# Output weights split during the last attention pair, in the room of the normed input, and the first token tile of the output projection multiplied there

## The reference

```python
# x: 1024 tokens x 1024, 16 learned meta tokens in front; everything in float32
z = rmsnorm(h, attn_norm)
q, k, v, f_logit, xc, b_gate, c_gate = split(z @ w_in)
attn = forgetting_attention(q, k, v, f_logit)          # 8 heads of 64
conv = b_gate * conv3(c_gate * xc)                      # short gated convolution, 512 wide
mixed = rmsnorm(concat(attn, conv) by groups of 64)     # 1024 wide
h = h + mixed @ w_out                                   # output projection
z = rmsnorm(h, ffn_norm)
h = h + hierarchical_moe(z)                             # 32 experts, 2 for each token
out = rmsnorm(h, final_norm)[16:]
```

## Time and profile before

| what | value |
|---|---|
| median of 3 runs | 1298.27 us (1297.89 to 1299.26) |
| the profiled execution | 1299.05 us, of which the span of the trace is 1297.1 us |
| PE, DVE, ACT busy | 1160.9, 888.4 and 738.7 us |
| block `output_projection` | 526.1 us to about 660 us of the span |
| expert block | from 660 us |

### The profile page before, as it was taken

The page is one execution under the profiler, slowest core; times in us unless marked ns, Lnnn a source line. Parts: engine busy times, 40 slices in busy tenths (PEclk is TensorE's granted clock), DMA queues, the critical chain, the costliest instruction groups (busy, mean ns, idle before and its releaser), DMA issues. The chain is left out here.

```text
span 1297.1 us, 17769 instructions
## 1 busy us (share of the span) xinstructions
PE 1160.9 (89%) x6109; PEld 907.2 (70%) x6109; DVE 888.4 (68%) x1117; ACT 738.7 (57%) x882; POOL 80.3 (6%) x135
## 2 busy tenths in 40 slices
PE   5999999999999997699949999999999999999950
PEld 3888788779878885588736667666667666676630
DVE  7445635553563454666659898888988889888838
ACT  7344444443444434522247777777777777777724
POOL 0011011011010000001200000000000000000013
PEclk8999999999999998899969999999999999999975
DMA  6145353345331000574369999999999999999928
GB/s 182 51 114 122 83 129 81 89 118 125 89 90 48 17 18 1 200 308 162 142 219 351 382 389 402 397 391 389 392 399 401 388 390 392 398 402 390 385 85 332
DMA packets 86214, 306.28 MB, mean 236 GB/s; under 512 B 14665, under 2 KB 39241, under 8 KB 61601
## 3 DMA queue, kind: packets, MB, share of 16 engines
q1 hardware_dynamic: 67680, 241.83, 49.4%
q0 software_dynamic: 11328, 38.80, 11.0%
q10 hardware_dynamic: 7168, 25.17, 5.8%
HBM read 254.36 MB, written 51.41 MB: 236 GB/s over the span
## 5 line engine op out<-in xcount | busy, mean ns | idle before, releaser
L1483 DVE TENSOR_TENSOR m_wl<-raw,m_wh 128x2048 fp32r<-128x2048 f32 x192 | 437.2, 2289 | 75.4 <-ACT m_wh L1356 73.1
L1356 ACT ACTIVATE m_wh<-raw 128x2048 fp32r<-128x2048 f32 x192 | 367.8, 1918 | 130.0 <-PE m_py L131 50.7
L129 PE MATMUL m_pg<-m_wh,m_xh 128*96 128x512 f32 x256 | 104.3, 407 | 6.2 <-DVE m_xl L1487 4.9
L143 PE MATMUL a_pj<-zh,a_wh 128*128 128x348 f32 (+1 forms) x416 | 107.6, 355 | 0.0
L143 PE MATMUL a_pj<-zl,a_wh 128*128 128x348 f32 (+1 forms) x416 | 107.5, 355 | 0.0
L143 PE MATMUL a_pj<-zh,a_wl 128*128 128x348 f32 (+1 forms) x416 | 106.4, 352 | 0.0
L129 PE MATMUL m_py<-m_wh,m_hh 128*96 128x512 f32 x256 | 103.2, 403 | 2.3 <-DVE m_hl L1512 2.3
L129 PE MATMUL m_pu<-m_wh,m_xh 128*96 128x512 f32 x256 | 102.7, 401 | 0.0
L131 PE MATMUL m_pg<-m_wh,m_xl 128*96 128x512 f32 x256 | 101.9, 398 | 0.0
L130 PE MATMUL m_pg<-m_wl,m_xh 128*96 128x512 f32 x256 | 101.6, 397 | 0.0
L130 PE MATMUL m_py<-m_wl,m_hh 128*96 128x512 f32 x256 | 101.4, 396 | 0.0
(11 more groups left out here) (241 smaller groups left out, 2107.0 us busy)
## 6 DMA issues: line engine op xcount, KB each, us to landing
raw<-in_w_gate_dram SPq DMA_DIRECT2D x64, 1024.0 KB, 10.1
raw<-in_w_up_dram SPq DMA_DIRECT2D x64, 1024.0 KB, 9.3
raw<-in_w_down_dram SPq DMA_DIRECT2D x64, 1024.0 KB, 8.7
xrows<-a_kl POOLq DMA_DIRECT2D x51, 256.0 KB, 4.9
a_raw<-in_w_in_dram SPq DMA_DIRECT2D x24, 512.0 KB, 4.1
m_xg<-xrows ACTq DMA_DIRECT2D x32, 384.0 KB, 8.2
yrows<-m_ys ACTq DMA_DIRECT2D x32, 384.0 KB, 7.0
yrows<-a_kl POOLq DMA_DIRECT2D x33, 256.0 KB, 4.9
```

Source lines behind the costliest of these rows:

```text
L129: nc.tensor.matmul(out, xh, wh, start=first, stop=False)
L143: mm = nc.tensor.matmul(out, w[:, k, 0:m], z[:, k, at:at + n], start=n_pass == 0, stop=n_pass == PASSES - 1)
L1356: nc.scalar.activation(wh[s][:], raw[j][:], ACT.Copy).then_inc(S["w_hi"], 1)
L1483: nc.vector.tensor_tensor(wl[s][:], raw[j][:], wh[s][:].bitcast(F32), ALU.subtract).then_inc(S["w_lo"], 1)
```

## The change

The split of `w_out` moves from the output block into the last pair of `mixers`, and so does the product of token tile 0. Its parts:

- The two slots `a_raw` of the mixers, free after the last projection weights are split, take the eight pieces of `w_out` one after the other (SP, issued by a wait for the slot's `out_lo`). `out_high(n)` on ACT writes piece `OUT[n]` into `zh`, `out_low(n)` on DVE the remainder into `zl`. They stand behind the split of each probability group in steps 15 and 16 (pieces 0 to 4) and behind step 16 (5, 6, 7).
- The token tile 0 of `mx` is split into `wh[0]` and `wl[0]`: the six old blocks in steps 15 and 16, the two own blocks at the end of the pair.
- `out_product(n)` on PE multiplies tile 0 by piece `OUT[n]` in six matmuls into the bank pair `pj`: 0 and 1 between the turned groups of step 16, 2 behind the spread in step 17, 3 to 7 at the end.
- `output_projection` takes `zh`, `zl`, `wh`, `wl` and `pj` over, and loads no `w_out`. Its PE begins with tile 1. Its SP now issues the six expert loads directly behind the small ones, ahead of the third tile of `o_x`; their buffers have new places.

```diff
 # mixers, SP, end of the last pair
+                    if final:
+                        for n, k in enumerate(OUT):
+                            if n < 2:
+                                sp.wait_ge(S["split_lo"], i * WT + (n + 7))
+                            else:
+                                sp.wait_ge(S["out_lo"], n - 1)
+                            sp.dma_start(out_raw(n), w_out[0, k * P:(k + 1) * P, :]).then_inc(out_in[n % 2], 16)
 # mixers, ACT
+                    def out_high(n):
+                        if final:
+                            act.wait_ge(S["projected"], i * WT + 8)
+                            act.wait_ge(out_in[n % 2], 16 * (n // 2 + 1))
+                            nc.scalar.activation(c.zh[:, OUT[n], 0:D], out_raw(n), ACT.Copy).then_inc(S["out_hi"], 1)
...
+                                if s >= STEPS - 1:
+                                    out_high(2 * (s - STEPS + 1) + a)
...
                         if s == STEPS:
+                            out_high(5)
...
+                            out_high(6)
+                            out_high(7)
...
+                    if final:
+                        act.wait_ge(S["conv_mixed"], 1)
+                        act.wait_ge(S["mixed"], i + 2)
+                        nc.scalar.activation(own_blocks(wh[0]), own_blocks(c.mx), ACT.Copy).then_inc(S["tile_hi"], 1)
 # mixers, DVE
+                    def out_low(n):
+                        if final:
+                            dve.wait_ge(S["out_hi"], n + 1)
+                            nc.vector.tensor_tensor(c.zl[:, OUT[n], 0:D], out_raw(n), c.zh[:, OUT[n], 0:D].bitcast(F32),
+                                                    ALU.subtract).then_inc(S["out_lo"], 1)
 # mixers, PE
+                    def out_product(n):
+
+                        if final:
+                            k = OUT[n]
+                            if n == 0:
+                                pe.wait_ge(S["gated"], i + 1)
+                            pe.wait_ge(S["tile_lo"], 1 if n < 6 else 2)
+                            pe.wait_ge(S["out_lo"], n + 1)
+                            for b in range(2):
+                                cols = slice(b * BANK, (b + 1) * BANK)
+                                three_passes(nc, pj[:, cols], wh[0][:, k, :], wl[0][:, k, :], c.zh[:, k, cols], c.zl[:, k, cols],
+                                             n == 0, n == KD - 1)
...
+                                if s == STEPS and a >= 1:
+                                    out_product(a - 1)
...
+                            out_product(2)
...
+                    for n in range(3, KD):
+                        out_product(n)
 # output_projection, SP
-                for k in range(SLOTS):
-                    weights(k)
                 for t in range(2):
                     sp.dma_start(xt[t][:], x[0, t * P:(t + 1) * P, :]).then_inc(x_in[t], 16)
-                for k in range(SLOTS, KD):
-                    weights(k)
...
+                for e, kind, j in [(0, 0, 2), (0, 1, 3), (0, 2, 4), (0, 3, 5), (1, 0, 0), (1, 1, 1)]:
+                    to, src = unit(c.raw[j], kind, e, w_gate, w_up, w_down)
+                    sp.dma_start(to, src).then_inc(c.raw_in[j], 16)
 # output_projection, PE
-                pe.wait_ge(S["m_lo"], 1)
-                for k in range(KD):
-                    pe.wait_ge(S["w_lo"], k + 1)
-                    for b in range(2):
-                        products(0, b, [k])
+                pe.sem_inc(S["multiplied"], 2)
```

More of the change, by code:

```diff
@@ L183, in mixers @@
         raw = [c.sb(ctx, f"a_raw{s}", [P, KD, P], F32) for s in range(2)]
-        wh = [c.sb(ctx, f"a_wh{t}", [P, KD, P], F32R) for t in range(2)]
-        wl = [c.sb(ctx, f"a_wl{t}", [P, KD, P], F32R) for t in range(2)]
+        wh, wl = c.wh, c.wl
         qs = c.sb(ctx, "a_qs", [P, 2, SEQ], F32R)
@@ L213, in mixers @@
         s3 = c.ps(ctx, "a_s3", [P, 3 * BANK])
-        pj = c.ps(ctx, "a_pj", [P, 3 * BANK])
+        pj = c.pj
         pt = c.ps(ctx, "a_pt", [P, BANK])
@@ L219, in mixers @@
                  "rden_done", "spread", "meta_kept", "o_scaled", "squared", "averaged", "rooted", "mixed", "cb_in", "taps_in",
-                 "x_copied", "u_done", "gated", "c_squared", "c_averaged", "c_rooted", "c_ln", "o_ln", "masks_made", "blanks_made", "own", "passed")
+                 "x_copied", "u_done", "gated", "c_squared", "c_averaged", "c_rooted", "c_ln", "o_ln", "masks_made", "blanks_made", "out_hi", "out_lo", "tile_hi", "tile_lo", "conv_mixed", "own", "passed")
         S = {n: c.sem("a_" + n) for n in names}
         raw_in = [c.sem(f"a_raw_in{s}") for s in range(2)]
+        out_in = [c.sem(f"a_out_in{s}") for s in range(2)]
         PIECES = 1 + NT
@@ L648, in pair @@
                                                       [P, NT, 2, HD])).then_inc(S["rden_done"], 1)
+                            for n in (5, 6, 7):
+                                out_low(n)
                             if not final:
@@ L663, in pair @@
                     dve.wait_ge(S["c_rooted"], i + 1)
-                    link(mix(cv, u, PAIRS))
+                    if final:
+                        mix(cv, u, PAIRS).then_inc(S["conv_mixed"], 1)
+                        dve.wait_ge(S["conv_mixed"], 1)
+                    else:
+                        link(mix(cv, u, PAIRS))
                     for n, (a, b) in sides(final):
@@ L1058, in place @@
                                     ALU.min).then_inc(S["placed"], 1)
[L1059 to L1064 removed]
+                dve.sem_inc(S["m_lo"], 1)
+                mix_low(1)
                 dve.wait_ge(S["made"], 1)
@@ L1180, in experts @@
         wl = [c.sb(ctx, f"{tag}_wl{s}", [P, UNIT], F32R) for s in range(RING)]
-        xg = [c.sb(ctx, f"{tag}_xg{s}", [BLK, D], F32) for s in range(2)]
         xh = [c.sb(ctx, f"{tag}_xh{s}", [P, KD * BLK], F32R) for s in range(2)]
         xl = [c.sb(ctx, f"{tag}_xl{s}", [P, KD * BLK], F32R) for s in range(2)]
+        over = c.sb(ctx, tag + "_over", [P, NE, NB_LESS], F32)
+        for j in range(UNITS):
+            c.sb(ctx, f"room_of_raw{j}", [P, UNIT], F32)
+        xg = [c.sb(ctx, f"{tag}_xg{s}", [BLK, D], F32) for s in range(2)]
         ids = [c.sb(ctx, f"{tag}_ids{s}", [BLK, 1], I32) for s in range(2)]
```

84 lines of the change are left out of this document (42 added, 42 removed).

## The result

The changed kernel takes 1305.35 us (median of 6 runs, 1304.29 to 1310.88), the kernel before 1298.04 (6 runs beside it, 1296.57 to 1299.26). The ratio is 1.0059, 95% interval 1.0044 to 1.0073: it is 0.59% slower, some 7.7 us by the ratio and 7.3 by the medians. I had forecast 1298.8 with a range up to 1302.5. The profiled execution took 1310.88, the longest of the six, and the one of the kernel before 1299.05: these two are 11.8 us apart, over 4 us more than the medians.

What follows compares the result with a forecast made beforehand. PE, busy 89% of the span, was taken as the bound, so its waits count. 15.5 us added in the last pair less 15.0 saved in the output block gave +0.5: 1298.8 us on the median, range 1293.5 to 1302.5.

Steps and rivals of the forecast that it cites:

- The tail: End of the last pair: `a_o` starts 8.8 us late, at 528.1, and the block change comes at 541.6.
- The 15.5 us added: Delay of the block change, from 526.1 to 541.6, by the added work, with five microseconds at half clock.
- the ring: Steps 15 and 16, where each turned group goes PE, ACT, DVE, PE; work put between the links delays it.
- the 3.3 us of a load: Last pair: time taken for one 512 KB load of a `w_out` piece on a quiet queue.
- What goes: Block change to tile 0's router logits (the mark): 27.57 us shrink to 12.6, so 15.0 us saved.
- second condition: Ahead of the mark, `o_wrg` waits for thirteen small loads, expected 11.5 to 12.5 us behind the block change.
- fall together: At the mark, PE's own work and the small loads are ready at about one time; 12.6 us taken.
- PE filled from there: Sign: from tile 0's logits on, PE has work without holes.
- The new buffers' places cost nothing: Output block: the moved buffers add no time.
- if PE stands for the small loads for over 2 us: Sign of being wrong, ahead of tile 0's logits: PE waits over 2 us for the thirteen small loads.
- The rival for slower: Two-slot ring: slower loads, some 2.4 us per microsecond, small loads 2 more; 1301 to 1304; chance 0.25.
- The rule that I set beside the ring: Two-slot loads: some 2.0 us fixed plus bytes, hidden only if issued early; chain 0.3 us shorter by it.

Runs made afterwards that it cites:

- e2: Changed kernel with the pieces of `w_out` landing in four places instead of two; 1304.12 us, ratio 1.0036 to the kernel before.
- e12: Changed kernel with five landing places and the splits of pieces 5 to 7 moved out of steps 15 and 16; 1299.50 us, ratio 1.0010.
- e3: Changed kernel with the six expert loads issued behind the first store of `o_z` again, as in the kernel before; 1304.29 us, ratio 1.0046.
- e8: Changed kernel with twelve small loads early, five landing places, late splits of pieces 5 to 7 and weight rows of 1024 columns; 1294.83 us, ratio 0.9962.
- e9: e8 with the high halves of the output weights starting 640 bytes further, at their old distance from the low halves; 1293.77 us, ratio 0.9966.
- e1: Changed kernel with twelve of the thirteen small loads issued in the last pair, into idle tiles; 1300.61 us, ratio 1.0008.
- e4: Changed kernel with tile 0's split and product moved back into the output block, weights still split in the last pair; 1307.59 us, ratio 1.0059.
- e11: Changed kernel with the eight loads of `o_gr` made one DMA; 1302.38 us, ratio 1.0028.
- e10: Changed kernel with the eight `o_gr` and two `o_br` loads issued ahead of the gain and the two `o_wr`; 1301.47 us, ratio 1.0020.
- e6: Changed kernel with the split weights in rows of 1024 columns instead of 1044; 1307.39 us, ratio 1.0069.
- e7: Changed kernel with twelve small loads early, four landing places and weight rows of 1024 columns; 1298.14 us, ratio 0.9990.
- e5: Kernel before with the output weights' halves in rows of 1044 columns instead of 1024; 1300.6 us, ratio 1.0011.

## Why the prediction was wrong

**The tail was right, to about 1 us.** Forecast: `a_o` near 528, block change 541.6, ACT's waits at pieces 2, 5 and 7, and a low clock behind the hole ahead of the averages. Measured: 527.86, 542.03, these waits and one more at piece 3 (0.77), the averages at 0.50 in 3.75 us. The 15.5 us added were 15.9. Counted from the previous addition of `a_o` (503.15, and 503.91 before) they were 16.7, and `a_o` was 9.3 us late where I had 8.8: the changed kernel's execution entered step 15 0.8 us early, which hides a part. Which part of the ring weighs most I had not said; e2 and e12 show it is the splits inside it more than their loads. The figures that I set beside the 3.3 us of a load, from the Trainium skill, DMA: Bandwidth & Descriptors, section Anatomy of one DMA, are there those of loads issued from GpSimd; these are issued on SP, and no term of the sum rested on them.

**The step that failed is "What goes", at its second condition:** "I expect 11.5 to 12.5, bounds 10.5 and 14.5" for the small loads, on the reasoning that eight pieces of `w_out` in front had stretched their issues. The pieces were not the cause, or not the main one. Without them the first `o_gr` is blocked for 3.79 us, and in the kernel before it was blocked nearly as long, 3.32, with the other seven at 0.43 each:

```profile
539.51 3.32 SPq L933 DMA_DIRECT2D o_gr<-in_ffn_norm_dram  x1
```

The last load lands 15.6 us behind the block change (11.3 until its issue and 4.3 to land, where the sum for "as long as before" had 10.9 and 3.6), beyond my bound, and the mark comes at 16.27 instead of 12.6: 3.7 us. PE itself was ready 10.5 us behind the block change (its last product starts at 552.16 and takes 0.39), since the clock stayed high there (1.00), so the two conditions that I let "fall together" were 5.75 us apart.

**A cost that had no term** followed from it. The stall lowered the clock to 0.50 for more than 8 us: 3.9 us more (17.84 against 13.92). I had the low level behind the block change, where it didn't come, and none behind the mark. "PE filled from there" held, at half speed.

**A cost put at nothing:** "The new buffers' places cost nothing" was wrong by some 0.2 us a tile, 1.1 us in all.

In the trace these make 15.9 - 27.57 + 16.27 = 4.6 at the mark, 3.9 and 0.2 for the clock and the first step, 1.0 until tile 7: 9.7. The medians are closer than these two executions, and what the others lost at each place no trace shows; e3, whose order of PE is the same, had a step of 16.79 and ended at 1303. The expert block is left out of this: between the last logits and the end the changed kernel's execution took 2.3 us longer than before, but with the same instructions there e8 took 2.6 us longer, e9 1.5 and e3 3.2 us less, so it varies with no visible link to the change.

My sign of being wrong, "if PE stands for the small loads for over 2 us", named the place. The rival for slower put 2 us there and most of its weight on the ring's loads; both its place and its price were off. The rule that I set beside the ring, from the Trainium skill, DMA: Bandwidth & Descriptors, section Rules for kernel authors (a load's fixed part is hidden where it is issued early and waited for late), bore more on the thirteen small loads. e1, which does that to twelve of them, agrees with 6.6 us, though most of what it takes out of the way is the time of the blocked issues (11.3 of the 15.6 us until the last one landed), which is not the fixed part.

## What to carry to other kernels

When work is taken out of a stage, list what that work covered. Thirteen small loads (0.5 to 512 KB) were free under 10.9 us of product and cost 5.75 us, and the clock behind them, when it was gone; issued some 110 us ahead of the block change, into tiles that are idle then, twelve of them are free again (e1). Splits that fill "idle" time belong behind the ring whose links wait for each other, not between them: the same three splits a few rows later were worth 0.26 to 0.28%, and places for their loads to land another 0.23%. And when an issue is seen to take eight times its usual length, find what blocks it before assuming that a change removes it.

## What the runs showed of the hardware that was not expected

- An issue on SP takes 0.43 us, but the first one behind the gain (512 KB) and the two `o_wr` (128 and 16 KB, in 1024 rows each) took 3.3 to 3.9 us in the kernel before, the changed one, e2, e3, e4, e11 and e12, whether or not `w_out` was in the queue. With the ten smallest ahead, none of the thirteen was over 1.5 us, and the load behind them took 2.28 (e10). Behind the two `o_wr` without the gain the longest took 1.60 (e1).
- A short stall was followed by a lower clock, also where PE had been full shortly before (5.00 of 5 us from 545 to 550 in e11): 1.25 us of idleness at the mark came with 1.6 us lost up to tile 1 (e11), 2.22 with 1.6 (e10), 2.89 with 1.6 (e2), 3.46 with 3.2 (e12), 4.65 with 2.9 (e3), 5.28 with 4.1 (e6), 5.75 with 3.9. Without a stall there, in e1, e4, e7, e8 and e9, nothing was lost. The 2.7 us at the block change sometimes lowered it (0.66 in e1) and sometimes not (1.00 in the changed kernel).
- The same 512-column matmuls take 1.5 to 1.7% longer for a tile with other places of their operands (13.72, 13.92 or 13.96 us). The row length of the weights alone does it in one place (e5), and shorter rows do not undo it in another (e6), where other operands have moved too.
